# Key branches of a sparse-attention stage: turns and values issued ahead of the samples, a lag of three steps, and a causal mask that opens its bank

## The reference, cut to what matters

```python
s = jnp.einsum('bqghd,bgqkd->bghqk', qg, kb) * scale
p = _masked_softmax(s, (kpos <= qpos[None, None, :, None])[:, :, None])
o_sel = jnp.einsum('bghqk,bgqkd->bqghd', p.astype(vb.dtype), vb)
...
s = jnp.einsum('bqghd,bkgd->bghqk', qg, kwin) * scale
p = _masked_softmax(s, wmask)
o_win = jnp.einsum('bghqk,bkgd->bqghd', p.astype(vwin.dtype), vwin)
```

## Time and profile before

| | us |
|---|---|
| median of 3 runs (1667.16 to 1671.71) | 1669.1 |
| the profiled execution | 1672.55 |
| its span, first to last instruction | 1670.8 |
| in it, the stage of the key branches, first matmul 1323.7 to last addition 1602.4 | 279 |
| PE busy over the whole span | 1452.4 |
| POOL busy over the whole span | 369.0 |

### The profile page before, as it was taken

How to read it: one execution, slowest core, us unless ns; L and a number is a source line. 1 busy time by engine, 2 the same in 40 slices (tenths; PEclk the granted TensorE clock), 3 DMA queues, 4 the chain that set the end, 5 groups by cost and what they waited for, 6 DMA issues and landing times. The chain is left out here.

```text
span 1670.8 us, 23376 instructions
## 1 busy us (share of the span) xinstructions
PE 1452.4 (87%) x9034; PEld 1084.8 (65%) x9050; DVE 741.7 (44%) x1370; ACT 544.5 (33%) x1123; POOL 369.0 (22%) x431
## 2 busy tenths in 40 slices
PE   6998859999999959999679899899999588878785
PEld 5887445553646429977557799899999344434354
DVE  1543142826446473334565444421222654554546
ACT  4111042141414123234544343332222144444433
POOL 5000033150504100000000332200000165566610
PEclk9999978998989889999879799898999589999988
DMA  5110024736364572212275431212214022221011
GB/s 169 51 51 0 6 76 143 261 127 219 139 246 152 177 276 103 102 67 101 101 254 183 139 107 40 97 56 101 102 51 101 26 80 74 77 76 51 27 66 54
DMA packets 92660, 180.80 MB, mean 108 GB/s; under 512 B 7255, under 2 KB 37235, under 8 KB 92371
## 3 DMA queue, kind: packets, MB, share of 16 engines
q1 hardware_dynamic: 80598, 129.04, 23.5%
q0 software_dynamic: 11952, 50.27, 8.4%
HBM read 133.45 MB, written 54.17 MB: 112 GB/s over the span
## 5 line engine op out<-in xcount | busy, mean ns | idle before, releaser
L2415 POOL TENSOR_SCALAR P<-P,rc 128x128 f32<-128x128 f32 (+3 forms) x128 | 136.8, 1086 | 119.4 <-DVE rc L2349 118.9
L1755 PE MATMUL ps<-axh,awh 128*128 128x288 f32 (+1 forms) x512 | 151.1, 295 | 7.7 <-DVE awl L1845 5.5
L1756 PE MATMUL ps<-axl,awh 128*128 128x288 f32 (+1 forms) x512 | 150.0, 293 | 0.0
L1757 PE MATMUL ps<-axh,awl 128*128 128x288 f32 (+1 forms) x512 | 149.3, 292 | 0.0
L348 PE MATMUL ps<-xnT,wring 128*128 128x288 f32 (+1 forms) x512 | 121.9, 400 | 1.1 <-PEq L2670 1.1
L895 DVE SCALAR_TENSOR_TENSOR wring<-wring,nbw,ps 128x512 f32<-128x512 f32 x128 | 88.4, 743 | 61.6 <-PE ps L639 59.1
L2301 ACT ACTIVATE P<-ps,nmx 128x128 f32<-128x128 f32 (+3 forms) x128 | 66.0, 528 | 148.5 <-DVE nmx L2338 148.5
L348 PEld LDWEIGHTS ps<-xnT,wring 128*128 128x128 f32 x512 | 98.9, 195 | 21.1 <-ACT xnT L269 1.2
L1845 DVE TENSOR_TENSOR awl<-wring,awh 128x1024 fp32r<-128x1024 f32 x32 | 39.3, 1227 | 156.8 <-ACT awh L1809 156.8
L1755 PEld LDWEIGHTS ps<-axh,awh 128*128 128x128 f32 x512 | 98.9, 193 | 8.0 <-DVE awl L1845 5.7
L1757 PEld LDWEIGHTS ps<-axh,awl 128*128 128x128 f32 x512 | 99.3, 194 | 0.0
(11 more groups left out here) (485 smaller groups left out, 3250.7 us busy)
## 6 DMA issues: line engine op xcount, KB each, us to landing
wring<-in_state_C_dram SPq DMA_DIRECT2D x32, 1024.0 KB, 5.9
out_dram<-wring POOLq DMA_DIRECT2D x32, 1024.0 KB, 5.1
wring<-in_a_w_up_dram SPq DMA_DIRECT2D x8, 2048.0 KB, 8.7
wring<-in_b_w_in_dram SPq DMA_DIRECT2D x8, 2048.0 KB, 8.0
wring<-in_a_w_down_dram SPq DMA_DIRECT2D x4, 2048.0 KB, 7.9
out_dram<-in_cache_win_dram POOLq DMA_DIRECT2D x8, 1016.0 KB, 15.8
wring<-in_w_kv_dram SPq DMA_DIRECT2D x3, 2048.0 KB, 7.7
arena<-in_cache_kv_dram SPq DMA_DIRECT2D x40, 128.0 KB, 2.8
```

Of the source, the lines that this page charges most:

```text
L1755: pe.matmul(out, w_hi, x_hi, start=kt == 0, stop=False)
L1756: pe.matmul(out, w_hi, x_lo, start=False, stop=False)
L1757: m = pe.matmul(out, w_lo, x_hi, start=False, stop=kt == KD - 1)
L2415: m = pool.tensor_scalar(p, p, rc[:, t % 2, gpar, a:a + 1], None, ALU.mult)
```

## The change

- The lag of `turn` behind `score` goes from two steps to three, that of `values` from three to four and that of the multiplication into `zT` from four to five; `P` gets a fourth buffer, and the loop one more round.
- PE issues turn and values right behind score, ahead of all pieces of the samples. ACT copies the turned bank right behind the exponentials, and DVE does divisors, its copy and the multiplication into `zT` right behind the maxima.
- In `score` the mask's products come first and open the bank (`start` on the first), and the score products add to them. For steps with several heads all masks come first, then all scores.
- In the samples' values, the 4 new rows' probabilities are no longer masked by parity: one copy into `sPn` in place of two into `sPz`, and 4 products in place of 8.
- Small tables move to other scopes or shrink (`cmask`, `ones`, `vecs1`), which makes room for the buffer.

```diff
-    NP, TURN, VALUES, MIX = 3, 2, 3, 4
+    NP, TURN, VALUES, MIX = 4, 3, 4, 5
...
-    sPz = sb("sPz", [128, 2, 5, 128])
+    sPz, sPn = sb("sPz", [128, 2, 4, 128]), sb("sPn", [S, 128])
...
-    END = NS + 8
+    END = NS + 9
...
-                x = eng.tensor_copy(mine(sPz[0:S, p, 4, :]), mine(b[0:S, 0:128]))
+            x = eng.activation(mine(sPz[:, p, :, :].rearrange("p r c -> p (r c)")), mine(b[:, :]), ACT.Copy)
+        if not par:
+            x = eng.tensor_copy(sPn[:, :], b[0:S, 0:128])
...
+            for gpar in range(2):
+                for a in range(s.nh):
+                    pe.matmul(b[:, gpar, s.w * a + s.w - 128:s.w * a + s.w], k.identb[:, :], k.causb[:, :], start=a == 0, stop=False,
+                              skip_group_check=True)
             for a in range(s.nh):
                 for gpar in range(2):
                     p0 = 64 * gpar
-                    pe.matmul(b[:, gpar, s.w * a:s.w * a + s.w], k.Qd[p0:p0 + 64, 4 * s.gp + s.h0 + a, 128 * s.i:128 * s.i + 128],
-                              k.KT[p0:p0 + 64, s.br - 1, s.gp, 0:s.w], start=True, stop=True)
-                for gpar in range(2):
-                    m = pe.matmul(b[:, gpar, s.w * a + s.w - 128:s.w * a + s.w], k.identb[:, :], k.causb[:, :], start=False, stop=True,
-                                  skip_group_check=True)
+                    m = pe.matmul(b[:, gpar, s.w * a:s.w * a + s.w], k.Qd[p0:p0 + 64, 4 * s.gp + s.h0 + a, 128 * s.i:128 * s.i + 128],
+                                  k.KT[p0:p0 + 64, s.br - 1, s.gp, 0:s.w], start=False, stop=True, skip_group_check=True)
...
@@ PE's loop
             if t < NS:
                 score(t)
+            if 0 <= t - TURN < NS:
+                turn(t - TURN)
+            if unit_at(t, VALUES):
+                values(t - VALUES)
             if (m := pair_at(t, LOADK)) is not None:
                 sample_keys(m, 0)
...
-            if 0 <= t - TURN < NS:
-                turn(t - TURN)
...
@@ ACT's loop
             if t < NS:
                 powers(t)
+            if 0 <= t - TURN < NS:
+                keep_turned(act, t - TURN, 1)
...
@@ DVE's loop
             if t < NS:
                 maxima(t)
+            if 0 <= t - 1 < NS:
+                divisors(t - 1)
+            if 0 <= t - TURN < NS:
+                keep_turned(dve, t - TURN, 0)
+            if (s := unit_at(t, MIX)):
+                dve.wait_ge(k.pv_full, s.u + 1)
+                z = k.zT[:, s.br, 4 * s.gp:4 * s.gp + 4, 128 * s.i:128 * s.i + 128]
+                dve.tensor_tensor(z, z, o_bank.rearrange("p (h t) -> p h t", h=HPG), ALU.mult).then_inc(k.o_free, 1)
```

More of the change, by code:

```diff
@@ L2127, in keep_sample @@
         b, free = full_bank(eng, k, ("sT" if par else "sTn", m))
-        for p in range(2):
+        for p in range(2 * par):
             def mine(t):
                 return t.rearrange("p (c a x) -> p c a x", a=2, x=16)[:, :, p, :]
-            if par:
-                x = eng.activation(mine(sPz[:, p, 0:4, :].rearrange("p r c -> p (r c)")), mine(b[:, :]), ACT.Copy)
-            else:
-                x = eng.tensor_copy(mine(sPz[0:S, p, 4, :]), mine(b[0:S, 0:128]))
+            x = eng.activation(mine(sPz[:, p, :, :].rearrange("p r c -> p (r c)")), mine(b[:, :]), ACT.Copy)
+        if not par:
+            x = eng.tensor_copy(sPn[:, :], b[0:S, 0:128])
         x.then_inc(free, 1)
@@ L2231, in sample_values @@
             for par in range(2):
-                for r in range(5):
-                    n = 128 if r < 4 else S
+                for r in range(4):
                     for gp in range(2):
@@ L2236, in sample_values @@
                             g, q0 = head_rows(gp, gpar)
-                            v = rawV[:, par, r, DH * g:DH * g + DH] if r < 4 else k.V[0:S, br - 1, NT, DH * g:DH * g + DH]
-                            x = pe.matmul(b[q0:q0 + 32, 0:DH], sPz[0:n, par, r, q0:q0 + 32], v,
-                                          start=par == 0 and r == 0, stop=par == 1 and r == 4)
+                            pe.matmul(b[q0:q0 + 32, 0:DH], sPz[:, par, r, q0:q0 + 32], rawV[:, par, r, DH * g:DH * g + DH],
+                                      start=par == 0 and r == 0, stop=False)
+            for gp in range(2):
+                for gpar in range(2):
+                    g, q0 = head_rows(gp, gpar)
+                    x = pe.matmul(b[q0:q0 + 32, 0:DH], sPn[:, q0:q0 + 32], k.V[0:S, br - 1, NT, DH * g:DH * g + DH],
+                                  start=False, stop=True)
             x.then_inc(full, 1)
@@ L2255, in _ @@
                 sample_scores(m)
-            if 0 <= t - TURN < NS:
-                turn(t - TURN)
             if (m := pair_at(t, TURNS)) is not None:
                 sample_turns(m)
-            if unit_at(t, VALUES):
-                values(t - VALUES)
             if (m := pair_at(t, OUT)) is not None:
@@ L2324, in _ @@
                 act.activation(sP[:, T:TA], b[:, 0:S], ACT.Exp, bias=snmx[:, 2:3], accum_out=ss[:, 1:2]).then_inc(free, 1)
-            if 0 <= t - TURN < NS:
-                keep_turned(act, t - TURN, 1)
             if (m := pair_at(t, TURNS)) is not None:
@@ L2370, in _ @@
                 dve.tensor_reduce(out=snmx[:, 2:3], in_=snmx[:, 0:2], axis=AX.X, op=ALU.max, negate=True).then_inc(k.smx_ready, 1)
[L2371 to L2374, removed]
             if (m := pair_at(t, TURNS)) is not None:
@@ L2400, in _ @@
                 x.then_inc(free, 1)
[L2401 to L2404, removed]
     @block.gpsimd
@@ L2501, in stage_attention @@
         k.QS = sb("QS", [128, 2, SB // 2, 2, 32], where=att)
-        k.cmask = sb("cmask", [128, NT, 32], where=att)
         k.identb = sb("identb", [128, 128], BF16, where=att)
@@ L2507, in stage_attention @@
         with ExitStack() as first:
+            k.cmask = sb("cmask", [128, NT, 32], where=first)
             k.tsel = sb("tsel", [S, SB // 2, 4, 8, HPG], where=first)
@@ L2649, in build @@
         k.ident = sb("ident", [128, 128])
-        k.ones = sb("ones", [128, 128])
+        k.ones = sb("ones", [128, 1])
         k.pages = sb("pages", [1, SB * 4], I32)
-        k.vecs1 = sb("vecs1", [128, 112])
         k.vecs2 = sb("vecs2", [128, 28])
@@ L2669, in build @@
             k.mask32 = sb("mask32", [128, 32], where=mlstm)
+            k.vecs1 = sb("vecs1", [128, 112], where=mlstm)
             with ExitStack() as c:
```

## The result

The changed kernel takes 1622.46 us (median of 4 runs, 1618.76 to 1624.26), the kernel before beside it 1668.13. The ratio is 0.9721 with a 95% interval of 0.9696 to 0.9745, so it is faster by some 46 us. The direction was forecast and so was the mechanism of the waits. The size was not: 27.7 us were forecast.

The account below looks back on a forecast made before the run. PE sets the stage's pace but idles a fifth of it, mostly in waits. Net 22.7 us from waits, 1 masks, 2 samples, 2 clock make 27.7: 1669.1 to 1641.4 us, range 1630 to 1652 (wide 1622 to 1660).

Parts of the forecast that it names:

- Part 1, the lag: Turns in the key branches' stage: a third step of lag removes their 18.4 us wait for POOL, no less than 14.
- Part 2, the ring: Three-bank ring: 28.8 us of waits removed, 24 new ones (bounds 12 and 40), from 5.9 to 6 a group in four.
- Part 3, the multiplication: Values after a four-step unit still wait for DVE's multiplication: 5.7 us in place of 5.2.
- Part 4, the masks: Masks ahead of scores on PE: net 1 us gained, bounds 4 gained and 3 lost.
- Part 5, samples: Samples' values: one of two runs of products with the new rows goes in each pair, 2 us gained.
- Part 6, the clock: PE's clock in the stage: one fall less in some groups, 2 us gained; bounds 8 gained and 3 lost.
- Ends and loads: Stage's start and end: waits for key loads unchanged at 3.9 us; half-speed last turn and values might gain 2 us, not counted.
- The rival of the loads: Shorter rounds make PE wait 3.9 us for loads in each of eight pairs: 1672.6 us; chance 0.05, shared with other no-change causes.
- its own signs: Turns' POOL waits only in last steps, bank waits near zero, about 24 us of copy waits, groups 58 to 60, 64 records.
- PE alone bounds: Rival for the stage: early copies and a clock that holds, waits put in 12 + 5.7, clock 8: 1620.4 us; chance 0.13.
- The ring takes the gain back: Rival: new ring waits of 40 us, no clock gain, masks at -3, leaving 5.7 us: 1663.4 us; chance 0.17.
- slower: Rival: samples' pieces waiting at BACK and LOADK hold up the next score; at 0.9 us each, 1692 us; chance 0.05.

Follow-up runs that it names:

- act_copy_first: The changed kernel with one swap: ACT copies the turned bank ahead of the exponentials; 1611.96 us, ratio 0.9673 to the kernel before.
- masks_single: The kernel before with masks first only in the 32 steps with one head; ratio 1.0004 to the kernel before.
- masks_multi: The kernel before with masks first only in the 12 steps with four or two heads; ratio 0.9955 to the kernel before.
- the base: The kernel before with only the samples' new rows unmasked by parity and the small tables moved; ratio 1.0004 to the kernel before.
- dve_copy_ahead: The changed kernel with turned banks copied earlier: ACT's ahead of exponentials, DVE's ahead of maxima; ratio 0.9723 to the kernel before.

## Why the prediction was right in kind and wrong in size

The step that failed is the term for the clock in the sum: "one fall less in some groups, 2 us in all". The profiles show 10.4 us (9.2 with PE's busy share as weight). The other mis-sized terms are the ring's new waits, 24 forecast and 14.8 measured, and the masks, whose own 2.3 us were near the 1 forecast but which brought half of the clock's gain. Most of these errors lie on the same side, and the forecast came out 18 us short.

**Bound.** PE's waits set the stage, as read. Lag and order removed 27.2 us of PE's idle time without the masks' help.

**Part 1, the lag.** Right: 18.4 us became 1.4. What the text did not say is that the lag needs the order and the order the lag. With the order alone this wait grows to 26.4.

**Part 2, the ring.** The mechanism was right and the replay close where it could be checked: 0.75 for 1.0, 1.98 for 1.8, 0.59 for 0.65 (LOADK in the sixth step), 0.31 for 0.3, and 0.36 and 0.49 for 0.7 and 0.5. One wait did not come in this group, 0.95 at LOADV of the second step (0.34 came in one other group). The clock had fallen there, and PE at half speed needs 1.7 us for the turns (1490.92 to 1492.67), in which DVE gets its copy done. In act_copy_first, at full clock, the wait is there:

```profile
1483.39 0.66 PE L2185 MATMUL ps<-ident,rawK 128*128 128x128 f32 x4 [1.26 <-DVE PT L2118]
```

The term was mis-sized, mostly by this and by "24 in four": the first group has no BACK of a pair before it, so three of the 1.8 us and not four.

**Part 3, the multiplication.** 5.7 forecast, 4.8 measured.

**Part 4, the masks.** I took 1 us gained, with bounds of 4 gained and 3 lost. The products alone give 0.8 us in each of 4 steps and some 0.2 in 8, a little over the upper bound, and cost 0.085 in each of 32 in the timelines: 2.3 net. The 2.4 us that 12 further changes between parts of the array and the full one should cost are not seen, but masks_single, with 3.3 us either way, can't exclude them. Where many such changes go, a step with four heads takes 1.65 us in place of 2.46 in the changed kernel and the same in masks_multi, thus 0.13 us for each of six changes, inside the 0.1 to 0.2 that I read. The Trainium skill ("TensorEngine Tiling (Array Packing)", Key Properties) says that a change of tiling mode drains TensorE. These steps agree with it. In the stage the masks are worth 6.9 us on top of the rest and 11.8 alone, and most of that is the clock, which this part did not cost at all.

**Part 5, samples.** 2 forecast, 3.0 in the profile without the clock, too little to show in the whole time.

**Part 6, the clock.** The step that failed. 10.4 us by the profiles (27.4 lost before, 17.0 after) against 2 forecast; the bounds, 8 gained and 3 lost, did not hold it either. I costed the clock by one stretch of a group. The experiments take the gain apart: the base loses 1.8 us more than the kernel before, lag and order together lose 7.0 less than the base (58.4 to 44.3), though either alone gave only 1.8, and the masks 5.2 less again (44.3 to 34.0). So the clock came back only when most of the waits were gone together. The forecast also looked at the groups alone: 7 of the 20.8 us of slow time that went lie in the first 36 us of the stage. Why the masks bring their share stays open.

**Ends and loads.** In the drain the last score is done at 1531.5, the last turn starts at 1540.95 and values at 1543.71, all at half speed as before:

```profile
1530.35 1.13 PE L2152 MATMUL ps<-KT,Qd 64*128 64x512 f32 x4
...
1538.46 1.07 PE L2164 MATMUL ps<-ident,P 128*128 128x128 f32 x8 [0.82 <-DVE PT L2118]
1540.95 1.97 PE L2164 MATMUL ps<-ident,P 128*128 128x128 f32 x8 [1.42 <-POOL P L2418]
1543.71 5.58 PE L2176 MATMUL ps<-PT,V 128*64 128x512 f32 x16 [0.79 <-DVE PT L2118]
```

The possible 2 us of gain there did not come. Loads cost 3.8 us more than before, where the prediction had them unchanged. The rival of the loads had 3.9 us in each of the eight pairs. Its mechanism came once, 2.13 us at the second pair, and no later LOADK waits for a load.

**The sum.** Stage: idle time 27.4 (22.7 forecast), clock 10.4 (2), samples 3.0 (2), masks' own products 2.3 by the timelines (1). That is 43.1 of 45.0 us. The remaining 1.9 are not accounted for, or 3.1 with the clock's 9.2. Of the 17 us between 27.7 and 45.0, the clock explains 8.4, waits 4.7, masks and samples 2.3.

Of its own signs, the waits of turns went as said and the 64 records of the new rows are there, but the group of 58 to 60 us came out at 54.2. The rival "PE alone bounds" (1620.4 us, chance 0.13) was the one that came true in its time and in two of its conditions, fewer waits and a better clock. It should have had more weight: its waits (12) were nearer to 14.8 than the forecast's 24, and its 8 us for the clock nearer than 2. "The ring takes the gain back" and "slower" were refuted for this change. dve_copy_ahead shows that one copy put at the wrong place costs 11.8 us of the stage.

## What to carry to other kernels

When PE sets the pace and stands still for a fifth of the time, a wait can have two prices: its length, and what the clock loses in the work behind it. Here the second was 5 us of the stage for three stalls of 2 us. Cost both, from rows at either level. Before moving a piece of work in a ring of few banks, look at what stands in front of the copy that frees the bank: a 0.6 us copy behind 2.8 us of exponentials was worth 10 us of stage, and putting it first was one swap in ACT's loop. Test the parts of such a change in pairs as well: lag and order gave 13.6 and 10.3 us alone and 36.9 together.

## What was unexpected of the hardware

With each step's mask products grouped ahead of its score products, and no other change, the granted clock in the stage was 0.93 in place of 0.90 and the time at half speed 36.0 us in place of 54.8, while PE's idle time stayed the same. Grouping them in twelve steps alone gave the same (35.8 us). These are single profiles; the mean clock of the runs rose by less, from 0.919 to 0.922 and from 0.920 to 0.922 over the whole span. And with the stalls of 2 us at BACK gone (act_copy_first), 177 us on end ran at 1.00, though PE still stood still for 18.5 us of them, up to 1.6 us at a time.
